# Branch gates with a 512-column product: the norm factor and the bias move from VectorE to GpSimd

## The chip, the cores and the metric

One Trainium2 chip, one core. The metric is device time in microseconds, the median of several runs of the whole program. PE is TensorE, ACT ScalarE, DVE VectorE, POOL GpSimd, SP the engine that issues most DMAs.

## What is computed

Three transformer blocks on 256 tokens of width 1024, in float32. The first one has two attention branches whose outputs are weighed by gates:

```python
h = _rmsnorm(x, g_mix[layer])
...
o_a = _stick_breaking_attention(...)
o_b = _diff_attention(q1, q2, k1, k2, vh, lam)
...
gates = jax.nn.sigmoid(jnp.einsum('bsd,de->bse', h, w_gate[layer]) + b_gate[layer])
gates = gates.reshape(b, s, N_BRANCH, D_MODEL)
merged = gates[:, :, 0] * br_a + gates[:, :, 1] * br_b
x = x + jnp.einsum('bsd,de->bse', merged, w_out[layer])
```

The change concerns the line with `gates`: 2048 output columns, computed as sixteen slabs of 128.

## The kernel before

The weights come as 319 slabs of 128x1024, through six slots (`stage`). For each slab ACT rounds it to a high half (`w_hi`, `next_hi`, L1058) and DVE subtracts to get the low half (`w_lo`, `next_lo`, L1490); the activations are split in the same way into `a_hi` and `a_lo`, which lie side by side in `a_pair`. A product is then the sum of three: high weights by high and by low activations, and low weights by high ones. `column_slab` (L496) does it with three matmuls of 256 columns for each of eight chunks, all into one half of a PSUM bank. `wide_slab` (L773), which the FFNs use, does the first two as one matmul of 512 columns over `a_pair`: the bank's first half then holds high by high plus low by high, the second half high by low, and someone has to add the halves. In the FFNs ACT copies the second half to SBUF (L1247) and DVE adds (L1701).

The gates run at L863 on PE: slab c goes to bank 4 or 2 in turn, and before slab c PE waits until the bank's earlier slab was taken out of it (`g_taken`). DVE (L1868 on) multiplies the bank by `rB`, the norm factor of each token, and adds the bias with a floor of -87 (L1883). After every second slab ACT turns two gates into sigmoids (`gates_out`, L1353: L1072, L1073, L1358), needed in the branch slabs that follow.

The differential attention is laid under the gates, as steps between slabs (`attend`, with the table `DA_AT`: head h starts at gate slab 1 + 3h). For a head, PE makes the scores (`da_scores`) after that slab; DVE takes row maxima (`da_max`, L1579, L1594); ACT the exponentials (`da_exp`, L1152); DVE normalizes and combines the two softmaxes (`da_probs`, L1600 to L1607) after its work on the gate of the next slab (for head 0 ahead of it, at slab 2); PE transposes (`da_turn`, L667) two slabs after the scores; then come the values, a sum of squares of the output (squared on POOL, L2094 and L2097), its norm on ACT, and the scaling on DVE (`da_out`, L1616). The order on each engine is that in which its block issues the instructions, with semaphores between the engines; no scheduler changes it.

Of the kernel before, what the change touches and what calls it, by code (L numbers as in the profile page):

```python
# [25 lines left out]
SLOTS = 6  # L26
# [28 lines left out]
V_BGATE = 64  # L55
# [40 lines left out]
def trunk(nc, xT_d, slab_d, vec_d, con_d, pos_d, out_d):  # L96
    f32, f32r, i32 = mybir.dt.float32, mybir.dt.float32r, mybir.dt.int32
    ALU, ACT = mybir.AluOpType, mybir.ActivationFunctionType
    with ExitStack() as ctx:
# [3 lines left out]
        def sem(name):  # L103
            return ctx.enter_context(nc.semaphore(name))
# [34 lines left out]
        def chunks(t, a, n):  # L139
# [66 lines left out]
                sem(n) for n in ("ds_done", "ds_taken", "ds_exp", "dp_ready", "dt_done", "dt_taken", "do_done",  # L206
                                 "do_taken", "dms_done", "dr_ready", "dn_ready", "do_hi", "do_lo"))
        down_done = sem("down_done")
        mix_ready, mhi_ready, mlo_ready = sem("mix_ready"), sem("mhi_ready"), sem("mlo_ready")
        acc_done = sem("acc_done")  # L210
        low_taken, gu_taken, gu_scaled, silu_ready, up_taken, ff_made, ffhi_ready, fflo_ready = (
# [38 lines left out]
        def half(b, i):  # L250
            return bank[b][:, i * TOK:(i + 1) * TOK]
# [192 lines left out]
        def _(pe):  # L444
# [418 lines left out]
            for c in range(16):  # L863
                n = GATE + c
                if c >= 2:
                    pe.wait_ge(g_taken, c - 1)
                else:
                    pe.wait_ge(qk_taken, 16)
                column_slab(n, n % SLOTS, half(GATE_BANK[c % 2], 0))
                if c < 2:  # L870
                    da_norm_sum(2 + c)
                attend(n)
# [157 lines left out]
        def _(act):  # L1030
# [329 lines left out]
            for c in range(16):  # L1360
                n = GATE + c
                if c == 1:
                    keys_factor(1)
                if c < 2:
                    pair_squares(2 + c)
                if c and c % 2 == 0:
                    gates_out(c - 2)
                next_hi(n)
                if c == 2:
                    queries_factor(1)  # L1370
                attend(n)
            gates_out(14)
            for s in range(8):
                attend(BRANCH + s)
                next_hi(BRANCH + s)
                j, side = branch(s)
                if side:
                    act.wait_ge(mix_ready, j + 1)
                    nc.scalar.activation(b_hi[:, 2 * j:2 * j + 2, :], gates[:, 2 * j:2 * j + 2, :], ACT.Copy
                                         ).then_inc(mhi_ready, 1)  # L1380
# [92 lines left out]
        def _(dve):  # L1473
# [394 lines left out]
            for c in range(16):  # L1868
                n = GATE + c
                attend_first(n)  # L1870
                next_lo(n)
                if c == 1:
                    normed_keys(1)
                if c == 2:
                    partners(0, 1)
                    da_probs(0)
                if c == 5:
                    partners(1, 1)
                dve.wait_ge(slab_done, n + 1)
                times(gates[:, c, :], half(GATE_BANK[c % 2], 0), rB[:, :]).then_inc(g_taken, 1)  # L1880
                dve.wait_ge(g_taken, c + 1)

                nc.vector.tensor_scalar(gates[:, c, :], gates[:, c, :], span(vec, V_BGATE + c, 1), -87.0, ALU.add,  # L1883
                                        ALU.max).then_inc(g_scaled, 1)
                attend(n)
                if c == 5:
                    rotated(0, 1)
                    rotated(1, 1)
# [173 lines left out]
        def _(pool):  # L2062
# [22 lines left out]
            for c in range(4):  # L2085
                for e in range(2):
                    pool.wait_ge(a_exp, 2 * c + e + 1)
                    below(soft_t[:, e, :]).then_inc(a_masked, 1)
            for h in range(4):

                pool.wait_ge(osq_made, h + 1)
                if h == 0:
# [2 lines left out]
                pool.wait_ge(osq_full, h + 1)  # L2095
                pool.wait_ge(do_taken, h + 1)
                nc.gpsimd.tensor_tensor(osq_lo, sq[:, 0:TOK], osq_hi.bitcast(f32), ALU.subtract).then_inc(osq_low, 1)  # L2097
            for m in range(1, 5):
                add_squares(add_index(m), 7, m + 1)
                if m == 1:  # L2100
# [134 lines left out]
```

## Time and profile before

| what | value |
|---|---|
| median of 3 runs | 1002.15 us (1001.6 to 1003.12) |
| the profiled execution | 1001.23 us |
| its span, from first to last instruction | 999.3 us |
| mean granted clock of TensorE | 0.998 |
| busy | PE 99%, DVE 73%, ACT 60%, POOL 6% |

The span lacks some 2 us of start and end that the time holds. The page's own sections give shares over the whole span; the gates take 57.6 us of it, from 95.7 to 153.3, so what happens there is read from timelines of that stretch.

### The profile page before, as it was taken

Reading aid. Unit: us, or ns where it says so; the run is one execution under the profiler, and the core shown is the slowest. Engines: PE = TensorE matmul, PEld = TensorE weight load, DVE = VectorE, ACT = ScalarE, POOL = GpSimd, SP = SyncE. Lnnn points to the kernel's source line nnn. Section 1 sums busy time; section 2 is a strip of 40 time slices with the busy share of each in tenths; the row PEclk is TensorE's granted clock in tenths of the full one; section 3 lists DMA queues with packets and bytes.
Section 4 is the critical chain, followed back from the end, with each engine's and each line's share of the span. In section 5 each row is a group of like instructions: output and inputs, shape, how many; then the busy total and the mean of one; then the engine's idle time right before and its main releaser. Section 6 shows DMA issues by size and latency. Waiting matters only on the chain.

```text
span 999.3 us, 17249 instructions
## 1 busy us (share of the span) xinstructions
PE 985.0 (99%) x6660; PEld 891.9 (89%) x6660; DVE 733.6 (73%) x1385; ACT 597.8 (60%) x1102; POOL 58.5 (6%) x78
## 2 busy tenths in 40 slices
PE   8999999999999999999999999999999999999996
PEld 7999989998888889999988888889989998888885
DVE  4668987798888548676498888647977688888644
ACT  5677785576566336565485555436668675565433
POOL 3011110020000002000020000002100010000000
PEclk9999999999999999999999999999999999999999
DMA  7743455456666764434546665753566456665731
GB/s 294 275 150 110 149 153 171 167 182 196 189 192 186 234 191 142 138 124 135 162 150 190 190 188 187 231 182 132 174 191 195 144 165 193 188 187 182 229 101 42
DMA packets 50928, 174.39 MB, mean 175 GB/s; under 512 B 6304, under 2 KB 8864, under 8 KB 50720
## 3 DMA queue, kind: packets, MB, share of 16 engines
q1 hardware_dynamic: 49664, 172.12, 54.3%
q10 hardware_dynamic: 1184, 1.18, 0.6%
q8 instruction: 53, 0.87, 0.4%
q14 instruction: 27, 0.22, 0.1%
HBM read 169.86 MB, written 1.05 MB: 171 GB/s over the span
## 4 chain that ended last, share of the span: by engine, by line
PE 95%; DVE 2%; ACT 1%; DMA 1%; issue 0%; SPq 0%; DVEq 0%; ACTq 0%
PE bank L446 93%; PE bank L667 1%; DMA stage<-slab_dram 1%; DVE w_lo L1490 1%; DVE arena L1483 0%; ACT w_hi L1058 0%; DVE soft_s L1579 0%; ACT soft_p L1152 0%; SPq L363 0%; DVE soft_p L1607 0%; DVE arena L1850 0%; ACT arena L1073 0%; DVE arena L1883 0%; ACT arena L1072 0%; DVE soft_p L1603 0%
## 5 line engine op out<-in xcount | busy, mean ns | idle before, releaser
L446 PE MATMUL bank<-a_pair,w_hi 128*128 128x512 f32 (+1 forms) x1968 | 532.6, 343 | 2.8 <-DVE w_lo L1490 2.1
L1490 DVE TENSOR_TENSOR w_lo<-stage,w_hi 128x1024 fp32r<-128x1024 f32 (+2 forms) x322 | 386.5, 1210 | 83.8 <-ACT w_hi L1058 79.2
L1058 ACT ACTIVATE w_hi<-stage 128x1024 fp32r<-128x1024 f32 (+2 forms) x314 | 325.6, 1043 | 165.7 <-PE bank L446 153.8
L446 PE MATMUL bank<-a_pair,w_lo 128*128 128x256 f32 x1488 | 416.8, 281 | 0.0
L446 PEld LDWEIGHTS bank<-a_pair,w_hi 128*128 128x128 f32 x1968 | 338.9, 189 | 51.3 <-DVE w_lo L1490 4.0
L446 PEld LDWEIGHTS bank<-a_pair,w_lo 128*128 128x128 f32 x1488 | 282.4, 190 | 0.0
L446 PE MATMUL bank<-arena_r,w_hi 128*128 128x256 f32 (+1 forms) x1024 | 237.0, 317 | 0.0
L446 PE MATMUL bank<-arena_r,w_lo 128*128 128x256 f32 x656 | 184.6, 282 | 0.0
L446 PEld LDWEIGHTS bank<-arena_r,w_hi 128*128 128x128 f32 x1024 | 168.7, 190 | 14.6 <-issue 1.4
L1247 ACT ACTIVATE arena<-bank 128x256 f32<-128x256 f32 x126 | 48.4, 384 | 136.4 <-PE bank L446 136.4
L446 PEld LDWEIGHTS bank<-arena_r,w_lo 128*128 128x128 f32 x656 | 125.0, 190 | 0.0
L1701 DVE TENSOR_TENSOR tmp<-bank,arena 128x256 f32<-128x256 f32 x126 | 53.5, 425 | 50.9 <-ACT arena L1247 44.2
L446 PE MATMUL bank<-ff_more,w_hi 128*128 128x512 f32 (+1 forms) x244 | 84.4, 392 | 0.0
L2076 POOL TENSOR_TENSOR sumsq<-sumsq,sq 128x256 f32<-128x256 f32 x47 | 38.1, 811 | 638.0 <-ACT sq L1079 587.2
L446 PE MATMUL bank<-ff_more,w_lo 128*128 128x256 f32 x240 | 67.3, 281 | 0.0
L1483 DVE TENSOR_TENSOR tmp<-tmp,rB 128x256 f32<-128x256 f32 x129 | 54.4, 422 | 4.3 <-ACT tmp L1238 2.2
L446 PEld LDWEIGHTS bank<-ff_more,w_hi 128*128 128x128 f32 x244 | 45.5, 188 | 10.7
L446 PE MATMUL bank<-w_hi,a_pair 128*128 128x256 f32 x256 | 47.7, 287 | 0.0
L446 PEld LDWEIGHTS bank<-ff_more,w_lo 128*128 128x128 f32 x240 | 45.4, 189 | 0.0
L446 PEld LDWEIGHTS bank<-w_hi,a_pair 128*128 128x128 f32 x256 | 39.8, 191 | 0.9 <-issue 0.6
L1579 DVE CUSTOM_DVE_ANT_0 soft_s<-bank,con 128x128 f32<-128x128 f32 x80 | 25.2, 355 | 15.5 <-PE bank L446 15.4
L446 PE MATMUL bank<-w_lo,a_pair 128*128 128x256 f32 x128 | 36.2, 282 | 0.0
(191 smaller groups left out, 776.2 us busy)
## 6 DMA issues: line engine op xcount, KB each, us to landing
stage<-slab_dram SPq DMA_DIRECT2D x319, 512.0 KB, 4.0
con<-con_dram SPq DMA_DIRECT2D x1, 1153.5 KB, 10.7
xT<-xT_dram SPq DMA_DIRECT2D x4, 256.0 KB, 5.4
arena<-arena ACTq DMA_DIRECT2D x1, 1024.0 KB, 8.8
arena<-tmp SPq DMA_DIRECT2D x32, 32.0 KB, 3.1
out_dram<-arena SPq DMA_DIRECT2D x3, 256.0 KB, 2.5
tmp<-arena SPq DMA_DIRECT2D x16, 16.0 KB
vec<-vec_dram SPq DMA_DIRECT2D x1, 213.5 KB, 11.5
```

The costliest lines, as they stand in the source:

```text
L446: return nc.tensor.matmul(out, lhsT, rhs, start=start, stop=True, skip_group_check=True)
L667: last = nc.tensor.transpose(b[:, i * P:(i + 1) * P], probs[:, i * P:(i + 1) * P], ident)
L1058: nc.scalar.activation(hi, raw, ACT.Copy).then_inc(hi_made, 1)
L1247: nc.scalar.activation(low[:, t % 4, :], half(GU_BANK[t % 8], 1), ACT.Copy).then_inc(low_taken, 1)
L1483: return nc.vector.tensor_tensor(out, a, b, ALU.mult)
L1490: return nc.vector.tensor_tensor(out, a, hi.bitcast(f32), ALU.subtract)
L1579: return nc.vector.tensor_tensor_reduce(out=s[:, cols], in0=b[:, cols], in1=con[:, mask + cols.start:mask + cols.stop], scale=1.0, scalar= ...
L1701: return nc.vector.tensor_tensor(out, half(GU_BANK[t % 8], 0), low[:, t % 4, :], ALU.add)
L2076: nc.gpsimd.tensor_tensor(sumsq[:, :], sumsq[:, :], sq[:, (i % 2) * TOK:(i % 2 + 1) * TOK], ALU.add).then_inc(sq_added, 1)
```

## The change

PE computes the gates with `wide_slab`. ACT copies the second half of the bank to `gates[:, c, :]` as soon as the slab is done (semaphore `g_low`), ahead of its `next_hi`. DVE adds the first half to it, one operation where it had two. POOL multiplies the sum by `rB` and adds the bias with the floor, in place; its work on the attention's squares becomes a function that is called between gates 3 and 4, 6 and 7, 9 and 10, 12 and 13. `gates_out` moves: it is called at odd slabs for the two gates up to c - 2, ahead of the copy; the last call comes after the first step of the branch slabs.

```diff
--- before.py
+++ after.py
@@ -206,6 +206,7 @@
                 sem(n) for n in ("ds_done", "ds_taken", "ds_exp", "dp_ready", "dt_done", "dt_taken", "do_done",
                                  "do_taken", "dms_done", "dr_ready", "dn_ready", "do_hi", "do_lo"))
         down_done = sem("down_done")
+        g_low, g_normed = sem("g_low"), sem("g_normed")
         mix_ready, mhi_ready, mlo_ready = sem("mix_ready"), sem("mhi_ready"), sem("mlo_ready")
         acc_done = sem("acc_done")
         low_taken, gu_taken, gu_scaled, silu_ready, up_taken, ff_made, ffhi_ready, fflo_ready = (
@@ -866,7 +867,7 @@
                     pe.wait_ge(g_taken, c - 1)
                 else:
                     pe.wait_ge(qk_taken, 16)
-                column_slab(n, n % SLOTS, half(GATE_BANK[c % 2], 0))
+                wide_slab(n, n % SLOTS, bank[GATE_BANK[c % 2]])
                 if c < 2:
                     da_norm_sum(2 + c)
                 attend(n)
@@ -1363,15 +1364,18 @@
                     keys_factor(1)
                 if c < 2:
                     pair_squares(2 + c)
-                if c and c % 2 == 0:
-                    gates_out(c - 2)
+                if c >= 3 and c % 2:
+                    gates_out(c - 3)
+                act.wait_ge(slab_done, n + 1)
+                nc.scalar.activation(gates[:, c, :], half(GATE_BANK[c % 2], 1), ACT.Copy).then_inc(g_low, 1)
                 next_hi(n)
                 if c == 2:
                     queries_factor(1)
                 attend(n)
-            gates_out(14)
             for s in range(8):
                 attend(BRANCH + s)
+                if s == 0:
+                    gates_out(14)
                 next_hi(BRANCH + s)
                 j, side = branch(s)
                 if side:
@@ -1876,12 +1880,9 @@
                     da_probs(0)
                 if c == 5:
                     partners(1, 1)
-                dve.wait_ge(slab_done, n + 1)
-                times(gates[:, c, :], half(GATE_BANK[c % 2], 0), rB[:, :]).then_inc(g_taken, 1)
-                dve.wait_ge(g_taken, c + 1)
-
-                nc.vector.tensor_scalar(gates[:, c, :], gates[:, c, :], span(vec, V_BGATE + c, 1), -87.0, ALU.add,
-                                        ALU.max).then_inc(g_scaled, 1)
+                dve.wait_ge(g_low, c + 1)
+                nc.vector.tensor_tensor(gates[:, c, :], half(GATE_BANK[c % 2], 0), gates[:, c, :], ALU.add
+                                        ).then_inc(g_taken, 1)
                 attend(n)
                 if c == 5:
                     rotated(0, 1)
@@ -2086,7 +2087,7 @@
                 for e in range(2):
                     pool.wait_ge(a_exp, 2 * c + e + 1)
                     below(soft_t[:, e, :]).then_inc(a_masked, 1)
-            for h in range(4):
+            def out_squares(h):
 
                 pool.wait_ge(osq_made, h + 1)
                 if h == 0:
@@ -2095,6 +2096,15 @@
                 pool.wait_ge(osq_full, h + 1)
                 pool.wait_ge(do_taken, h + 1)
                 nc.gpsimd.tensor_tensor(osq_lo, sq[:, 0:TOK], osq_hi.bitcast(f32), ALU.subtract).then_inc(osq_low, 1)
+
+            for c in range(16):
+                if c in (4, 7, 10, 13):
+                    out_squares(c // 3 - 1)
+                pool.wait_ge(g_taken, c + 1)
+                nc.gpsimd.tensor_tensor(gates[:, c, :], gates[:, c, :], rB[:, :], ALU.mult).then_inc(g_normed, 1)
+                pool.wait_ge(g_normed, c + 1)
+                nc.gpsimd.tensor_scalar(gates[:, c, :], gates[:, c, :], span(vec, V_BGATE + c, 1), -87.0, ALU.add,
+                                        ALU.max).then_inc(g_scaled, 1)
             for m in range(1, 5):
                 add_squares(add_index(m), 7, m + 1)
                 if m == 1:
```

ACT's order at gate slabs 5 and 6. Just ahead of these rows stand the exponentials of head 1 (L1152 before, L1153 now). L1072, L1073 and L1358 (now one more each) are `gates_out`, L1058 (L1059) is the high half of a weight slab, L1159 (L1160) takes the transposes of head 1. Before:

```order
L1152 ACTIVATE soft_p,small<-soft_s,small 128x256
L1058 ACTIVATE w_hi<-stage 128x1024 [waits loaded5,slab_done]
L1072 ACTIVATE arena<-arena 128x512 [waits g_scaled]
L1073 ACTIVATE arena<-arena 128x512 [waits act_step]
L1358 ACTIVATE arena<-arena 128x512 [waits act_step]
L1058 ACTIVATE w_hi<-stage 128x1024 [waits loaded0,slab_done]
```

Now; L1370 is the copy of the bank's second half, first for slab 5, then for slab 6:

```order
L1153 ACTIVATE soft_p,small<-soft_s,small 128x256
L1073 ACTIVATE arena<-arena 128x512 [waits g_scaled]
L1074 ACTIVATE arena<-arena 128x512 [waits act_step]
L1359 ACTIVATE arena<-arena 128x512 [waits act_step]
L1370 ACTIVATE arena<-bank 128x256 [waits slab_done]
L1059 ACTIVATE w_hi<-stage 128x1024 [waits loaded5,slab_done]
L1370 ACTIVATE arena<-bank 128x256 [waits slab_done]
L1059 ACTIVATE w_hi<-stage 128x1024 [waits loaded0,slab_done]
```

`gates_out` (the three rows of 128x512) now comes directly after the exponentials and ahead of the copy for slab 5; before, no row of this engine stood between the slab and DVE's work on it.

DVE's order at gate slab 5. Before; L1483 into `arena` is the multiply by `rB`, L1883 the bias, L1600 to L1607 are `da_probs` of head 1:

```order
L1490 TENSOR_TENSOR w_lo<-stage,w_hi 128x1024 [waits hi_made]
L1483 TENSOR_TENSOR tmp<-tmp,con 128x512 [waits rot_done1]
L1483 TENSOR_TENSOR arena<-bank,rB 128x256 [waits slab_done]
L1883 TENSOR_SCALAR arena<-arena,vec 128x256 [waits g_taken]
L1600 RECIPROCAL small<-small 128x4 [waits ds_exp]
L1601 TENSOR_SCALAR small<-small 128x2 [waits dve_step]
L1603 TENSOR_SCALAR soft_p<-soft_p,small 128x128
L1603 TENSOR_SCALAR soft_p<-soft_p,small 128x256
L1607 SCALAR_TENSOR_TENSOR soft_p<-soft_p,small 128x128 [waits dve_step]
L1607 SCALAR_TENSOR_TENSOR soft_p<-soft_p,small 128x256
```

Now; L1884 is the add, L1604 to L1611 are `da_probs`:

```order
L1494 TENSOR_TENSOR w_lo<-stage,w_hi 128x1024 [waits hi_made]
L1487 TENSOR_TENSOR tmp<-tmp,con 128x512 [waits rot_done1]
L1884 TENSOR_TENSOR arena<-bank,arena 128x256 [waits g_low]
L1604 RECIPROCAL small<-small 128x4 [waits ds_exp]
L1605 TENSOR_SCALAR small<-small 128x2 [waits dve_step]
L1607 TENSOR_SCALAR soft_p<-soft_p,small 128x128
L1607 TENSOR_SCALAR soft_p<-soft_p,small 128x256
L1611 SCALAR_TENSOR_TENSOR soft_p<-soft_p,small 128x128 [waits dve_step]
L1611 SCALAR_TENSOR_TENSOR soft_p<-soft_p,small 128x256
```

The bias row is gone, and the operation on the gate waits for `g_low`, which ACT's copy raises, in place of `slab_done`; `da_probs` stands behind it as before.

## Rows read from the trace of the kernel before

**Rows 1.** The page: busy time of each engine, and the chain that ended last.

```profile
PE 985.0 (99%) x6660; PEld 891.9 (89%) x6660; DVE 733.6 (73%) x1385; ACT 597.8 (60%) x1102; POOL 58.5 (6%) x78
...
PE 95%; DVE 2%; ACT 1%; DMA 1%; issue 0%; SPq 0%; DVEq 0%; ACTq 0%
```

**Rows 2.** View by windows, the stretch of the gate slabs: us, then busy us (instructions) by engine.

```profile
95.70:153.30 57.60, 55.49 (x449) 52.06 (x448) 52.26 (x125) 45.67 (x96) 7.10 (x9) 1.00 0.47 147
```

**Rows 3.** PE's timeline (start us, us): after each head's scores, and its transposes (L667).

```profile
112.22 0.92 PE L446 MATMUL bank<-soft_t,arena 128*128 128x256 f32 x4
...
118.73 0.49 PE L667 MATMUL bank<-con,soft_p 128*128 128x128 f32 x3
...
123.13 0.92 PE L446 MATMUL bank<-soft_t,arena 128*128 128x256 f32 x4
...
131.60 0.55 PE L667 MATMUL bank<-con,soft_p 128*128 128x128 f32 x3 [1.80 <-DVE soft_p L1607]
...
136.05 0.92 PE L446 MATMUL bank<-soft_t,arena 128*128 128x256 f32 x4
...
143.03 0.55 PE L667 MATMUL bank<-con,soft_p 128*128 128x128 f32 x3 [0.31 <-DVE soft_p L1607]
```

**Rows 4.** PE's timeline: first and next line after the first gate slab.

```profile
92.85 0.40 PE L446 MATMUL bank<-a_pair,w_hi 128*128 128x256 f32 x2
...
95.73 1.02 PE L446 MATMUL bank<-sq,con 128*128 128x512 f32 x2
```

**Rows 5.** PE's timeline: starts of two 512-column lines one FFN slab apart.

```profile
299.75 0.39 PE L446 MATMUL bank<-a_pair,w_hi 128*128 128x512 f32 x1
...
302.52 0.39 PE L446 MATMUL bank<-a_pair,w_hi 128*128 128x512 f32 x1
```

**Rows 6.** Groups of instructions by line; the POOL ones by source line (ns min/median/max).

```profile
L1247 ACT ACTIVATE arena<-bank 128x256 f32<-128x256 f32 x126 | 48.4, 384 | 136.4 <-PE bank L446 136.4
...
L1701 DVE TENSOR_TENSOR tmp<-bank,arena 128x256 f32<-128x256 f32 x126 | 53.5, 425 | 50.9 <-ACT arena L1247 44.2
...
L1883 DVE TENSOR_SCALAR arena<-arena,vec 128x256 f32<-128x256 f32 x16 | 6.1, 380 | 0.6
...
L2094 POOL TENSOR_TENSOR sq<-o_raw x4: 614/616/1383, 114.0 to 148.1; 128x256 f32<-128x256 f32 x4
...
L2066 POOL TENSOR_SCALAR_AFFINE_SELECT soft_t<-soft_t x8: 404/832/1511, 56.7 to 94.6; 128x256 f32<-128x256 f32 x8
```

**Rows 7.** ACT's timeline: ends of the exponentials (L1152), and `gates_out` between 117.12 and 119.04.

```profile
116.08 0.19 ACT L1152 ACTIVATION_READ_ACCUMULATOR soft_p<-soft_s,small 128x1 f32 x1
...
117.12 0.62 ACT L1072 ACTIVATE arena<-arena 128x512 f32<-128x512 f32 x1
...
119.04 1.05 ACT L1058 ACTIVATE w_hi<-stage 128x1024 fp32r<-128x1024 f32 x1
...
129.65 0.19 ACT L1152 ACTIVATION_READ_ACCUMULATOR soft_p<-soft_s,small 128x1 f32 x1
...
140.46 0.19 ACT L1152 ACTIVATION_READ_ACCUMULATOR soft_p<-soft_s,small 128x1 f32 x1
```

**Rows 8.** DVE's timeline: `da_probs` of head 1, two splits, first maximum of head 2.

```profile
116.78 0.17 DVE L1600 RECIPROCAL small<-small 128x4 f32<-128x4 f32 x1
...
117.70 0.75 DVE L1607 SCALAR_TENSOR_TENSOR soft_p<-soft_p,small 128x128 f32<-128x128 f32 x2
...
121.08 1.22 DVE L1490 TENSOR_TENSOR w_lo<-stage,w_hi 128x1024 fp32r<-128x1024 f32 x1
...
126.18 0.28 DVE L1579 CUSTOM_DVE_ANT_0 soft_s<-bank,con 128x128 f32<-128x128 f32 x1
...
138.91 1.76 DVE L1490 TENSOR_TENSOR w_lo<-stage,w_hi 128x1024 fp32r<-128x1024 f32 x1
```

**Rows 9.** POOL's timeline: the operation beside the second of these splits.

```profile
138.72 0.87 POOL L2097 TENSOR_TENSOR arena_r<-sq,arena_r 128x256 fp32r<-128x256 f32 x1
```

## Prediction

> **What bounds the kernel now.** Read the engine shares and the chain that ended last first [rows 1]: PE is busy 99% of the span and holds 95% of the chain. So the kernel ends sooner only if PE gets less to do, or waits less. DVE at 73% and ACT at 60% of the whole span look idle, but such a share is a mean over stages. The stretch of the sixteen gate slabs, taken alone from the view by windows, reads otherwise [rows 2]: in 57.6 us PE is busy 55.5, DVE 52.3 and ACT 45.7; POOL 7.1. There PE has 2.1 us of idle time, and DVE is nearly full.
>
> Where the 2.1 us lie is seen in PE's timeline [rows 3]. The differential attention runs under the gates, one head per three slabs: PE does the scores of head h after gate slab 1 + 3h, DVE takes the row maxima, ACT the exponentials, DVE normalizes (`da_probs`), and two slabs later PE transposes the result (L667). The transposes of head 2 stood 1.80 us idle, those of head 3 0.31 us, both released by the last line of `da_probs`. Head 1 came without a wait. These three loops decide the stage; everything behind it is PE's own pace, so what the stage gains or loses is kept.
>
> **The change, part by part.**
>
> *The wide form.* The first gate slab takes 95.73 - 92.85 = 2.88 us on PE [rows 4]; a slab of an FFN, already in the wide form, 302.52 - 299.75 = 2.77 us [rows 5]. Both have the same columns; 16 weight loads stand for 24. Sixteen times 0.11 is **1.8 us** off PE's own work.
>
> *ACT's new copy.* Sixteen more copies of 128x256 from PSUM; the FFN's copy of that form takes 0.38 us [rows 6], so 6.1 us on an engine with 57.6 - 45.7 = 11.9 us free. As a load it fits. What counts is its place. ACT's queue is in order, and in the changed order, at slab 5 (and 11), it is exponentials of the head, then `gates_out`, then the copy. DVE's add waits for that copy, and behind the add in DVE's queue stands `da_probs`, for which PE's transposes wait. Before, DVE's first gate operation waited for the slab alone, and `gates_out` ran beside `da_probs`.
>
> *The loops, one by one.* For each: from the end of the scores on PE, how long PE has work of its own until the transposes (two wide slabs save 0.22 us of it), and how long the others take.
>
> Head 1. PE: 118.73 - 112.22 = 6.51 [rows 3], now 6.3. The others: exponentials end at 116.08 + 0.19 = 116.27 [rows 7], 4.05 after the scores; `gates_out` 119.04 - 117.12 = 1.92 [rows 7]; the copy 0.38 [rows 6]; DVE's add 0.43 [rows 6]; `da_probs` 117.70 + 0.75 - 116.78 = 1.67 [rows 8]. Sum 8.45, so PE waits **2.2 us** where it waited none.
>
> Head 2. At slab 8 no `gates_out` stands ahead of the copy. PE: 131.60 - 1.80 - 123.13 = 6.67 [rows 3], now 6.45. The others: exponentials end at 129.84, 6.71 after the scores [rows 3, 7], as DVE began the maxima only at 126.18 [rows 8], 3.05 us after the scores; then 0.38 + 0.43 + 1.67. Sum 9.2 less what DVE catches up: three tensor-scalars of 0.38 [rows 6] fewer between, 1.1, of which new holds by POOL (below) eat part; I take 0.6, between 0 and 1.1. PE waits **2.1 us** in place of 1.80.
>
> Head 3. PE: 143.03 - 0.31 - 136.05 = 6.67, now 6.45 [rows 3]. The others: exponentials end at 140.65, 4.60 after [rows 7], then 1.92 + 0.38 + 0.43 + 1.67. Sum 9.0: PE waits **2.5 us** in place of 0.31.
>
> Head 0. Its `da_probs` stands ahead of the add, so nothing new precedes it. But PE comes up to 0.4 us earlier (four shorter slabs) and the probabilities do not: between 0 and 0.4, I take **0.3 us**.
>
> *DVE's part.* Multiply and tensor-scalar become one add: 16 x 0.38 = 6.1 us less DVE work [rows 6]; the add takes the time of the multiply. Beyond head 2's 0.6 us I give nothing for it, since DVE now stands and waits for the copy.
>
> *POOL's part.* Sixteen multiplies: POOL's 128x256 multiply of two SBUF operands takes 0.62 in the median [rows 6]. Sixteen tensor-scalars, of which no row shows one: the nearest with one source, the affine select of 256 elements, goes from 0.40 to 1.51 [rows 6]; I take 0.6, near the multiply, the row of the same shape. With four pairs of squares that is some 25 us of 57.6: beside other work, if it is on time. `gates_out` at slab 5 needs POOL's result of slab 3, asked for two slabs, 5.5 us, earlier: hidden. Without this cover each late result would stand in full in the chain above.
>
> *POOL against DVE.* This is not free. The split that DVE began at 138.91, under POOL's operation at 138.72 [rows 9], took 1.76 us, against 1.22 for the one at 121.08 [rows 8]: an operation on two SBUF operands on DVE is held by some 0.5 us when it meets one of POOL. The new multiply is released by the add, just as `da_probs` begins behind it. For heads 1 to 3 I add 0.3 us each, between 0 and 1.0 (both POOL operations met): **0.9 us**. The Trainium skill says it more strongly ("SBUF — State Buffer", section "Who interferes with whom"): the port pair of DVE and GpSimd is an exclusive lock, whoever issues first has it for the whole instruction and the other fully blocks. The rows agree: the split ran its own 1.22 us from about the end of POOL's operation, 139.59, on. By that rule all 32 POOL operations could hold DVE, which is the third rival below; my sum does not need it.
>
> SP, the loads and the splits: the copies push `next_hi` by 0.38 us, but a high half is made six slabs ahead of its use; the DMA queue's order is untouched. Nothing.
>
> **Sum.** New waits 0.3 + 2.2 + 2.1 + 2.5 + 0.9 = 8.0; less the old waits 2.1; less 1.8: **+4.1 us**. The profiled execution took 1001.23 and becomes 1005.3; it stands 0.9 below the median of the three runs, 1002.15, so against the median **1006.3 us**. With the terms at their ends, the waits go from 0 + 2.2 + 1.6 + 2.0 + 0 = 5.8 (head 3 with 0.5 less, as 4.60 holds other ACT work) to 0.4 + 2.2 + 2.7 + 2.6 + 3.0 = 10.9: 1004.1 to 1009.2 for this case alone.
>
> **The rivals.**
>
> *The copies come in time* (faster). It decides at slabs 5, 8 and 11: if the copy is done before DVE would reach its add, no wait is new, and the 6.1 us taken from DVE remove the lateness of 3.05 us that made the wait of 1.80. Then 1.8 + 2.1 = 3.9 us go: 998.3. For it: DVE is the fullest engine behind PE. Against it: ACT's order, in which 1.92 us of `gates_out` stand between exponentials and copy. 0.12.
>
> *One wait covers the next* (no change). A wait at head 1 lets ACT and DVE catch up, so that head 3, and the holds by POOL, cost nothing more: 0.3 + 2.2 + 2.1 - 3.9 = +0.7, 1002.9. For it: head 3 waited only 0.31 after head 2's 1.80. Against: each loop begins anew with PE's scores. 0.16.
>
> *DVE held by POOL becomes the bound.* If each of the 32 POOL operations holds DVE for its 0.62 us, DVE has 52.3 - 6.1 + 19.8 = 66 us of work in a stage of 57.6: 8.4 more, 1010.5. For it the lengthened split [rows 8]; against it DVE's many operations that read PSUM, and its idle time at the adds. By the rule of the skill's SBUF page named above the trace agrees on the hold, and no run here shows how often it meets. 0.14.
>
> *POOL falls behind.* With 1.51 us for its tensor-scalar, 0.62 for its multiply and a hold of up to one split, 1.2 us, for each gate, POOL needs 3.3 us, and its squares 0.3 per slab (two operations for four heads in sixteen slabs): the stage's whole 3.6 us per slab; then `gates_out` waits for POOL, 1.5 us at each of three heads: 4.5 more, 1010.8. 0.08.
>
> **How the numbers follow.** My case has 0.50. About 0.2%, 2 us, is what a measurement of this kernel tells from no change. Faster: the first rival, 0.12. Same: the second, and the low end of mine, 0.18. Slower: the rest, 0.70. The range leaves out the first rival and the top of the last two: 1001.5 to 1010.5.
>
> **What would show it.** Right: the gate stretch longer by 3 to 6 us; waits at L667 of about 2 us for heads 1, 2 and 3, released by `da_probs`; DVE's add idle before it until ACT's copy, by about 2 us at slabs 5 and 11; slabs 0.11 us shorter. Wrong: no L667 waits, or the waits at the slabs' own first matmuls (then the bank's release is the bound, not the heads); POOL's tensor-scalar over 1 us, or ACT idle before `gates_out` until POOL.

## The result, and the profile after

The changed kernel took 1006.79 us in the median of 10 runs (1003.46 to 1008.11), the kernel before 1001.88 on the same chip. The ratio on record is 1.0057 (the quotient of the two medians is 1.0049), with a 95% interval of [1.004, 1.0074]: slower, by 0.4 to 0.7%. The profiled execution took 1005.53 us, with a span of 1003.8.

The page of the changed kernel, engine shares and chain by engine, to be held against [rows 1]:

```profile
PE 985.8 (98%) x6532; PEld 886.2 (88%) x6532; DVE 730.8 (73%) x1369; ACT 602.8 (60%) x1118; POOL 99.2 (10%) x110
...
PE 95%; DVE 2%; ACT 1%; DMA 1%; issue 0%; SPq 0%; DVEq 0%; ACTq 0%
```

The chain reads as before. POOL went from 58.5 to 99.2 us, nearly 41 more. Nothing here says where the time went; that takes the stage's own timeline. It shows PE at the end of gate slab 0 (`sq,con`), at the transposes of heads 1 to 3 (L668, before L667), two steps of the slab behind head 2's, and the head 3 product that ends the stage (`arena_r`):

```profile
95.50 1.02 PE L447 MATMUL bank<-sq,con 128*128 128x512 f32 x2
...
120.58 0.55 PE L668 MATMUL bank<-con,soft_p 128*128 128x128 f32 x3 [2.00 <-DVE soft_p L1611]
...
133.77 0.55 PE L668 MATMUL bank<-con,soft_p 128*128 128x128 f32 x3 [0.77 <-DVE soft_p L1611]
...
134.74 0.40 PE L447 MATMUL bank<-a_pair,w_hi 128*128 128x512 f32 x1
...
136.86 0.40 PE L447 MATMUL bank<-a_pair,w_hi 128*128 128x512 f32 x1
...
147.27 0.55 PE L668 MATMUL bank<-con,soft_p 128*128 128x128 f32 x3 [2.62 <-DVE soft_p L1611]
...
156.89 0.28 PE L447 MATMUL bank<-arena_r 128*128 128x256 f32 x1
```

From 95.50 to 156.89 are 61.39 us. The same two landmarks stood 57.21 us apart before (95.73 and 152.94): **the stage is 4.18 us longer**. Head 1, which came without a wait, now waits 2.00; head 2 0.77 in place of 1.80; head 3 2.62 in place of 0.31 [rows 3]. Together 5.39 us of waits against 2.11.

One part of the loss is not a wait. Between the transposes of head 1 and of head 2, without the wait, lie 133.77 - 0.77 - 120.58 = 12.42 us; the same work from head 2 to head 3 takes 147.27 - 2.62 - 133.77 = 10.88. The view by windows around head 1's wait says why (columns: window, length, busy time of PE, PEld, DVE, ACT and POOL, granted clock, DMA share, GB/s):

```profile
118.60:120.60 2.00, 0.02 (x1) 0.02 (x1) 1.97 (x6) 1.56 (x3) 1.90 (x2) 1.00 0.00 0
120.60:122.00 1.40, 1.40 (x9) 1.31 (x10) 1.37 (x3) 0.83 (x2) 0.06 (x1) 0.92 0.00 0
122.00:124.00 2.00, 2.00 (x8) 1.71 (x8) 1.97 (x3) 1.84 (x5) 0.00 (x0) 0.50 0.00 0
124.00:125.00 1.00, 1.00 (x5) 0.81 (x5) 1.00 (x3) 0.38 (x1) 0.20 (x1) 0.50 0.00 0
```

After PE stood idle for 2 us, its granted clock went from 1.00 to 0.50, which is the lower level (1.2 GHz), for some 3 us. PE counts as fully busy there and does less: 12.42 - 10.88 = **1.54 us** lost to the clock.

So the stage's 4.18 us are 5.39 - 2.11 = 3.28 of new waits and 1.54 of clock, less 0.64 by which PE's own work is shorter (57.21 - 2.11 = 55.10 before, 61.39 - 5.39 - 1.54 = 54.46 now). This says where PE's time went, not what each part cost: had the clock stayed up, PE would have come to head 2's transposes earlier, and might have waited there instead. The filling below answers that.

Why head 1 waits is read in the queues. ACT from the end of head 1's exponentials (L1153) through `gates_out` (L1073 to L1359) to the copy (L1370):

```profile
115.62 0.19 ACT L1153 ACTIVATION_READ_ACCUMULATOR soft_p<-soft_s,small 128x1 f32 x1
115.72 0.62 ACT L1073 ACTIVATE arena<-arena 128x512 f32<-128x512 f32 x1
...
117.09 0.63 ACT L1359 ACTIVATE arena<-arena 128x512 f32<-128x512 f32 x1
117.63 0.37 ACT L1370 ACTIVATE arena<-bank 128x256 f32<-128x256 f32 x1
```

DVE over the same time, the add (L1884) and the normalization of head 1 behind it, then POOL's multiply beside it:

```profile
118.03 0.42 DVE L1884 TENSOR_TENSOR arena<-bank,arena 128x256 f32<-128x256 f32 x1 [1.75 <-ACT arena L1370]
118.37 0.17 DVE L1604 RECIPROCAL small<-small 128x4 f32<-128x4 f32 x1
118.57 0.71 DVE L1605 TENSOR_SCALAR small<-small 128x2 f32<-128x2 f32 x1
...
119.77 0.76 DVE L1611 SCALAR_TENSOR_TENSOR soft_p<-soft_p,small 128x128 f32<-128x128 f32 x2
```

```profile
118.54 0.72 POOL L2104 TENSOR_TENSOR arena<-arena,rB 128x256 f32<-128x256 f32 x1 [0.42 <-DVE arena L1884]
```

The exponentials are done at 115.81. DVE could normalize then, but its next instruction is the add, which stands idle for 1.75 us until the copy, and the copy stands behind `gates_out`. The probabilities are ready at 120.53, 4.72 us after the exponentials. Head 3 shows the same with an idle time of 2.47 at its add. The L1605 of 0.71 us lies beside POOL's multiply and ends with it (119.28 and 119.26); at head 0, and at all four heads before the change, it takes 0.23. So `da_probs` takes 120.53 - 118.37 = 2.16 us in place of 1.67 [rows 8]; from the same timeline, 2.22 at head 2 and 2.16 at head 3.

POOL's two operations in the groups of the same kernel over the whole span, and four lines of its waits between 95 and 165 us (columns: who waited for whom, us in total, times, longest):

```profile
L2106 POOL TENSOR_SCALAR arena<-arena,vec 128x256 f32<-128x256 f32 x16 | 20.9, 1308 | 1.6
L2104 POOL TENSOR_TENSOR arena<-arena,rB 128x256 f32<-128x256 f32 x16 | 20.0, 1252 | 16.3 <-DVE arena L1884 16.3
```

```profile
POOL arena L2104 <- DVE arena L1884: 16.3, 9, 4.1
DVE arena L1884 <- ACT arena L1370: 12.2, 9, 3.4
...
PE bank L668 <- DVE soft_p L1611: 5.4, 3, 2.6
...
ACT arena L1073 <- POOL arena L2106: 3.3, 3, 2.4
```

POOL takes 2.56 us for a gate, over twice the 1.22 that the prediction took from the nearest rows [rows 6]. It was still mostly in time: ACT waited for it 3.3 us in all.

### The profile page after: what moved, and what is told of

It reads as the page before. It is cut to its first block, busy times and chain, and to the rows that moved or that the text cites. A ratio compares the mean times of both kernels' runs of the same rounds, so it can differ in the third digit from the quotient of the medians.

```text
span 1003.8 us, 17025 instructions
## 1 busy us (share of the span) xinstructions
PE 985.8 (98%) x6532; PEld 886.2 (88%) x6532; DVE 730.8 (73%) x1369; ACT 602.8 (60%) x1118; POOL 99.2 (10%) x110
## 4 chain that ended last, share of the span: by engine, by line
PE 95%; DVE 2%; ACT 1%; DMA 1%; issue 0%; SPq 0%; DVEq 0%; ACTq 0%
PE bank L447 93%; PE bank L668 1%; DMA stage<-slab_dram 1%; ACT soft_p L1153 1%; DVE soft_s L1583 0%; DVE soft_p L1611 0%; DVE arena L1487 0%; ACT arena L1370 0%; SPq L364 0%; DVE small L1605 0%; DVE soft_p L1607 0%; DVE arena L1884 0%; DVE w_lo L1494 0%; ACT arena L1074 0%; ACT arena L1073 0%
## 5 line engine op out<-in xcount | busy, mean ns | idle before, releaser
L1059 ACT ACTIVATE w_hi<-stage 128x1024 fp32r<-128x1024 f32 (+2 forms) x314 | 325.4, 1043 | 156.9 <-PE bank L447 144.4
L447 PEld LDWEIGHTS bank<-a_pair,w_hi 128*128 128x128 f32 x1840 | 323.9, 189 | 56.2 <-DVE w_lo L1494 3.8
```

What stands on the lines that cost most here:

```text
L447: return nc.tensor.matmul(out, lhsT, rhs, start=start, stop=True, skip_group_check=True)
L1059: nc.scalar.activation(hi, raw, ACT.Copy).then_inc(hi_made, 1)
```

## The experiments

Three causes were set against each other. The **queue** theory (Q): the copy stands behind `gates_out` on ACT and ahead of the heads' normalization on DVE. The **port** theory (P): POOL's operations hold DVE. The **clock** theory (C): the waits lower PE's clock, which costs time of its own. "At the transposes" means PE at L668, for one head after the other.

What the unchanged rest of the program takes is not constant. From the end of the stage to the end of the span it was 843.2 to 845.8 us in four of the twelve profiled executions (the heads first, POOL left out, the filling, the bias alone on POOL) and 846.0 to 848.4 in the other eight, both kernels of the change among them. So single spans are not compared here. The stage's length and the waits carry the argument; the medians are given with their intervals, and a difference of 2 or 3 us between two kernels can come from the rest.

### The changed kernel once more

No edit.

> The changed kernel once more, on the chip of the three that follow, so that they have a common base: 4 to 6 us over the kernel before; waits at the transposes of heads 1 to 3 of about 2, 0.8 to 2.5 and 2.5 us, with the lower clock behind one of the first two of them.

Measured: 1006.38 us, ratio 1.0051 [1.0034, 1.0068]. The waits repeat to 0.2 us. Behind head 1's wait the clock falls again, and from head 1 to head 2 PE takes 133.72 - 0.60 - 120.61 = 12.51 us. Behind head 3's wait it falls too, as it did not in the first execution. PE's transposes of heads 1 to 3 and the end of the stage, then three windows, one behind head 1's wait and two behind head 3's:

```profile
120.61 0.89 PE L668 MATMUL bank<-con,soft_p 128*128 128x128 f32 x3 [2.00 <-DVE soft_p L1611]
...
133.72 0.55 PE L668 MATMUL bank<-con,soft_p 128*128 128x128 f32 x3 [0.60 <-DVE soft_p L1611]
...
147.24 0.55 PE L668 MATMUL bank<-con,soft_p 128*128 128x128 f32 x3 [2.63 <-DVE soft_p L1611]
...
158.42 0.40 PE L447 MATMUL bank<-arena_r 128*128 128x256 f32 x2
```

```profile
122.00:124.00 2.00, 2.00 (x7) 1.69 (x7) 1.97 (x3) 1.94 (x5) 0.00 (x0) 0.50 0.00 0
...
147.80:149.00 1.20, 1.20 (x6) 1.00 (x6) 1.20 (x3) 1.14 (x3) 0.26 (x1) 0.57 0.00 0
149.00:151.00 2.00, 2.00 (x9) 1.71 (x8) 0.79 (x1) 1.88 (x4) 1.90 (x2) 0.50 0.78 231
```

After the same wait of 2.6 us the clock stayed at 1.00 in the first execution, and the stretch from head 3 to the end took 156.89 - 147.27 = 9.62 us; here it fell to 0.50 and the stretch took 158.42 - 147.24 = 11.18, 1.56 more. The whole stage took 62.84 us, against 61.39. What the waits cost through the clock differs from one execution of the same program to the next.

### Taking the heads out from behind the copy

First edit: `da_probs` of heads 1 to 3 ahead of the add.

```diff
-                    if n - lag in at and (step is not da_probs or at[n - lag]):
+                    if n - lag in at and step is not da_probs:
...
+                if c in (5, 8, 11):
+                    da_probs((c - 2) // 3)
                 dve.wait_ge(g_low, c + 1)
                 nc.vector.tensor_tensor(gates[:, c, :], half(GATE_BANK[c % 2], 0), gates[:, c, :], ALU.add
...
```

> In the changed kernel da_probs of heads 1 to 3 is called ahead of the add of that slab; nothing else differs. Theory Q (the queues: the copy stands behind gates_out on ACT and ahead of da_probs on DVE): the waits at the transposes of heads 1 and 3 (2.00 and 2.62 us) fall under 0.4 us, head 2 keeps about 1 us from DVE's lateness, the lower clock after head 1 is gone; about 999.5 us, 2 to 3 us under the kernel before. Theory P (DVE held by POOL's operations): the POOL operations are all there, waits of 1.5 us or more stay, at best 1 us under the changed kernel, 1005 to 1007.

Measured: 999.64 us, ratio 1.0014 [0.9997, 1.0031]. The stage takes 56.77 us, 4.6 less than with the change alone. PE's waits after 112 us in this kernel:

```profile
130.73 0.55 PE L668 MATMUL bank<-con,soft_p 128*128 128x128 f32 x3 [1.65 <-DVE soft_p L1611]
...
141.91 0.55 PE L668 MATMUL bank<-con,soft_p 128*128 128x128 f32 x3 [0.30 <-DVE soft_p L1611]
153.14 0.47 PE L447 MATMUL bank<-arena_r,w_hi 128*128 128x256 f32 x2 [0.59 <-issue]
159.94 0.50 PE L447 MATMUL bank<-arena_r,w_hi 128*128 128x256 f32 x2 [0.81 <-DVE arena L1487]
```

Heads 1 and 3 are back to what they were before the change (no wait and 0.31), as the queue theory has it, and the clock stays at 1.00. From head 2 to head 3 PE takes 141.91 - 0.30 - 130.73 = 10.88 us, which is the price of that stretch at full clock. All of POOL's operations are still there, so this run also speaks against the port theory, which had the waits of the changed kernel stay: of those over 1.5 us only head 2's is left, and that one was there before the change. The gain over the kernel before that was expected did not come: two waits behind the stage, 0.59 and 0.81, take some of it. The second is POOL's lateness, seen at ACT's last `gates_out` but one (L1073) and DVE's last add (L1886):

```profile
155.41 0.63 ACT L1073 ACTIVATE arena<-arena 128x512 f32<-128x512 f32 x1 [3.63 <-POOL arena L2108]
```

```profile
157.73 0.43 DVE L1886 TENSOR_TENSOR arena<-bank,arena 128x256 f32<-128x256 f32 x1 [3.36 <-ACT arena L1370]
```

ACT waits 3.63 us for POOL's bias, the copy of slab 15 stands behind it, and DVE's add behind that.

Second edit: on ACT the copy ahead of `gates_out`.

```diff
-                if c >= 3 and c % 2:
-                    gates_out(c - 3)
                 act.wait_ge(slab_done, n + 1)
                 nc.scalar.activation(gates[:, c, :], half(GATE_BANK[c % 2], 1), ACT.Copy).then_inc(g_low, 1)
+                if c >= 3 and c % 2:
+                    gates_out(c - 3)
```

> In the changed kernel ACT's copy is issued ahead of gates_out at odd slabs; da_probs stays behind the add. Theory Q: 1.9 us of gates_out leave the loops of heads 1 and 3, whose waits fall from 2.00 and 2.62 to about 0.1 to 0.7 us each; head 2 waits 1 to 2.4 us; about 1001.5 us, between 1000 and 1003. Theory P: waits as in the changed kernel, 1006 to 1007.

Measured: 1001.03 us, ratio 1.0025 [1.0007, 1.0043]; the stage 59.06. At the transposes: head 1 none, head 2 2.51, head 3 0.69. After head 2's wait the granted clock is 0.76 in the window 130 to 135 us and 0.90 in the next. The transposes of heads 2 and 3:

```profile
131.95 0.55 PE L668 MATMUL bank<-con,soft_p 128*128 128x128 f32 x3 [2.51 <-DVE soft_p L1611]
...
145.13 0.55 PE L668 MATMUL bank<-con,soft_p 128*128 128x128 f32 x3 [0.69 <-DVE soft_p L1611]
```

Between them PE takes 145.13 - 0.69 - 131.95 = 12.49 us where it takes 10.88 at full clock. So the order on ACT alone removes head 1's wait and most of head 3's (2.00 and 2.62 with the change alone), from the other end of the same chain; head 2, ahead of whose copy no `gates_out` stands, is not helped by it, and waits a little more than the 1 to 2.4 us expected.

Both edits together:

> The changed kernel with da_probs of heads 1 to 3 ahead of the add and ACT's copy ahead of gates_out. Theory Q, with what e1_probs_first left: heads 1 and 3 without a wait, head 2 with 1.5 to 2.5 us, and the wait of 0.81 us in the branch slabs gone, since copy and add of slab 15 no longer stand behind the gates_out that waited 3.6 us for POOL; 0.5 to 2 us under the kernel before. If POOL's lateness in itself sets the end of the stage (theory L): the wait in the branch slabs stays, 1 to 2 us over before, as e1_probs_first.

Measured: 1001.68 us, ratio 1.0006 [0.999, 1.0022]; the stage 56.14, with one wait left at the transposes, head 2's 1.67, and two behind the stage, 0.49 and 0.40. The gain of 0.5 to 2 us over the kernel before that was expected did not come, and the wait behind the stage fell by half instead of going. The interval overlaps that of the first edit alone: the second adds nothing that can be told. With the clock at 1.00 all the way, the stage less its wait is 56.14 - 1.67 = 54.47 us, the same as the 54.46 worked out for the changed kernel.

### POOL left out

The multiply and the bias go back to DVE, behind the add; POOL does nothing for the gates.

```diff
                                         ).then_inc(g_taken, 1)
+                dve.wait_ge(g_taken, c + 1)
+                times(gates[:, c, :], gates[:, c, :], rB[:, :]).then_inc(g_normed, 1)
+                dve.wait_ge(g_normed, c + 1)
+                nc.vector.tensor_scalar(gates[:, c, :], gates[:, c, :], span(vec, V_BGATE + c, 1), -87.0, ALU.add,
+                                        ALU.max).then_inc(g_scaled, 1)
                 attend(n)
...
-                pool.wait_ge(g_taken, c + 1)
-                nc.gpsimd.tensor_tensor(gates[:, c, :], gates[:, c, :], rB[:, :], ALU.mult).then_inc(g_normed, 1)
-                pool.wait_ge(g_normed, c + 1)
-                nc.gpsimd.tensor_scalar(gates[:, c, :], gates[:, c, :], span(vec, V_BGATE + c, 1), -87.0, ALU.add,
-                                        ALU.max).then_inc(g_scaled, 1)
```

> The changed kernel with the multiply and the bias back on DVE, behind the add; POOL does nothing for the gates; copy and order on ACT as changed. Theory Q: the waits at heads 1 and 3 stay at 2 us or more, since the copy stands where it stood, and DVE has 0.9 us more per slab; 1006 to 1009. Theory P: DVE's lines have their plain length again, the waits fall to those of the kernel before or less, 1003 or under.

Measured: 1010.01 us in the median of four runs, ratio 1.0121 [1.0083, 1.0158]; somewhat over the 1006 to 1009 expected. PE's waits from 95 to 165 us, and three windows, each behind one of them:

```profile
PE bank L668 <- DVE soft_p L1611: 10.4, 4, 3.7
```

```profile
125.00:130.00 5.00, 5.00 (x27) 3.94 (x26) 4.86 (x9) 3.30 (x6) 0.00 (x0) 0.76 0.33 102
...
140.00:145.00 5.00, 5.00 (x30) 4.01 (x29) 2.81 (x7) 1.83 (x5) 0.00 (x0) 0.89 0.64 201
...
155.00:160.00 5.00, 5.00 (x22) 4.33 (x22) 2.72 (x6) 3.48 (x7) 0.00 (x0) 0.69 0.68 181
```

The four heads wait 0.88, 3.73, 2.07 and 3.70 us and the clock falls three times. Had POOL's holds been what the change costs, and more than what POOL takes off DVE (P), this kernel would have been the better one. It is the worst of all. Two things differ in it, though: the holds are gone, and DVE's multiply and bias stand in the heads' chain too, 0.42 and 0.35 us unheld. So it shows that POOL's part is worth more than its holds cost; that the holds don't make the waits is shown by the first edit above.

The same with the heads taken out of the chain (this edit and the first one above):

> As e1_probs_first, but the multiply and the bias stay on DVE and POOL does nothing for the gates: the wide product with its copy and its order repaired. Asked is what POOL's part is worth. DVE has 0.8 us more per slab than in e1_probs_first, and 0.45 more than before: head 1 without a wait, head 2 with 2.5 to 4 us from DVE's lateness, 2 to 5 us over the kernel before. If POOL's work costs more than it frees (theory P): faster than e1_probs_first.

Measured: 1004.57 us, ratio 1.004 [1.0022, 1.0058], against 1.0014 [0.9997, 1.0031] with POOL; the intervals overlap, the waits are plain. At the transposes 0.88, 0.34, 3.33 and 0.43 us, of which those of heads 2 and 3:

```profile
135.19 0.90 PE L668 MATMUL bank<-con,soft_p 128*128 128x128 f32 x3 [3.33 <-DVE soft_p L1611]
...
147.91 0.55 PE L668 MATMUL bank<-con,soft_p 128*128 128x128 f32 x3 [0.43 <-DVE soft_p L1611]
```

Head 2, the one that depends on DVE's load and not on the copy, waits 3.33 without POOL and 1.65 with it.

### Keeping PE busy through the waits

Ahead of the transposes of heads 1 to 3, PE does twelve more products of 256 columns into an unused bank; their results are used nowhere.

```diff
             def da_turn(h):
+                if h:
+                    for _ in range(12):
+                        mm(half(3, 0), a_hi[:, 0, 0:P], a_hi[:, 1, :], True)
                 pe.wait_ge(dp_ready, h + 1)
```

> The changed kernel with 12 extra matmuls of 128x256 into an unused bank ahead of the transposes of heads 1 to 3 (results unused, about 1.4 us each time), so that PE works during most of the wait. Asked is what the lower clock after head 1 cost. Theory Q: the clock stays at 1.00, but head 2's loop is set by DVE and ACT, so its wait, 0.77 us beside the lower clock, becomes about 1 us more than the filling, and the time stays within 1 us of the changed kernel, 1006 to 1007. If the lower clock is a cost of its own (theory C): 1.7 us less, 1005 or under.

Measured: 1002.11 us, ratio 1.003 [1.0014, 1.0046]. PE from the filling ahead of head 1's transposes on:

```profile
118.50 1.59 PE L447 MATMUL bank<-a_pair 128*128 128x256 f32 x12
120.78 0.55 PE L668 MATMUL bank<-con,soft_p 128*128 128x128 f32 x3 [0.69 <-DVE soft_p L1614]
```

All windows of the stage have a granted clock of 1.00, and the transposes come when they came in the changed kernel: 120.78, 133.73 and 147.21, against 120.58, 133.77 and 147.27. The stage takes 61.28 us against 61.39. So in the profiled execution of the changed kernel the lower clock behind head 1 cost nothing in the end: head 2's transposes waited for DVE either way, and the 1.54 us stood in place of a longer wait. Between heads 1 and 2 the filled kernel takes 133.73 - 0.65 - 120.78 = 12.30 us, of which 12.30 - 10.88 = 1.42 are filling; with the 0.65 that is a wait of 2.07 us for head 2, had nothing filled it. A fall behind head 3, as in the repeated execution, has no such wait behind it and adds its 1.56 us in full.

In the median this kernel is 0.27% better than the change alone (1.003 against 1.0057; the intervals overlap a little, and those of the repeated run, 1.0051 [1.0034, 1.0068], more). That is not shown to be the clock's doing (C): the two profiled stages are equally long, and the profiled executions differ behind the stage, 843.3 us here against 846.9. What the lower clock costs in the median stays open.

### The narrow form, and how much POOL should do

Now the change without its 512-column form: three products of 256 columns, no copy on ACT, DVE only moves the bank out, POOL multiplies and adds the bias.

```diff
-                wide_slab(n, n % SLOTS, bank[GATE_BANK[c % 2]])
+                column_slab(n, n % SLOTS, half(GATE_BANK[c % 2], 0))
...
-                act.wait_ge(slab_done, n + 1)
-                nc.scalar.activation(gates[:, c, :], half(GATE_BANK[c % 2], 1), ACT.Copy).then_inc(g_low, 1)
...
-                dve.wait_ge(g_low, c + 1)
-                nc.vector.tensor_tensor(gates[:, c, :], half(GATE_BANK[c % 2], 0), gates[:, c, :], ALU.add
-                                        ).then_inc(g_taken, 1)
+                dve.wait_ge(slab_done, n + 1)
+                nc.vector.tensor_copy(gates[:, c, :], half(GATE_BANK[c % 2], 0)).then_inc(g_taken, 1)
```

> The half of the change that moves work to POOL, alone: narrow products, no copy on ACT; DVE moves the bank to SBUF in one operation, POOL scales and adds the bias, gates_out as in the changed kernel. Theory Q: without the copy no loop is longer; DVE is freed of one operation per slab; head 2's wait 0.5 to 2 us; from 1.5 us under to 0.5 us over the kernel before. Theory P (DVE held by POOL): waits at heads 1 to 3 of 1.5 us or more, 3 us or more over before.

Measured: 1000.39 us, ratio 0.9984 [0.997, 0.9999]; the stage 55.89. The whole loss of the change is gone with the wide form and its copy, and its place is taken by a small gain: head 2 waits 1.01, the others not at all. The stage's PE work, 55.89 - 1.01 = 54.88, is 0.4 us more than the 54.47 of the kernel with both edits, and no more than the 56.77 - 1.65 - 0.30 = 54.82 of the one with the heads first. So the wide form is worth 0.4 us here at most, or 0.6 against the 55.10 of the kernel before.

DVE's move of the bank takes 0.41 us, its multiply of the same size 0.42. So DVE may multiply as it did before, and POOL does the bias alone:

```diff
-                nc.vector.tensor_copy(gates[:, c, :], half(GATE_BANK[c % 2], 0)).then_inc(g_taken, 1)
+                times(gates[:, c, :], half(GATE_BANK[c % 2], 0), rB[:, :]).then_inc(g_taken, 1)
...
                 pool.wait_ge(g_taken, c + 1)
-                nc.gpsimd.tensor_tensor(gates[:, c, :], gates[:, c, :], rB[:, :], ALU.mult).then_inc(g_normed, 1)
-                pool.wait_ge(g_normed, c + 1)
                 nc.gpsimd.tensor_scalar(gates[:, c, :], gates[:, c, :], span(vec, V_BGATE + c, 1), -87.0, ALU.add,
...
```

> Three matmuls of 256 columns per chunk and no copy on ACT, as in the kernel before; DVE multiplies the bank by rB itself, as before, and POOL does the bias alone; gates_out stands where the change put it. Against the kernel of experiment e7 this takes the multiply (0.73 to 1.72 us each) from POOL and leaves DVE as it was there (a multiply of 0.43 for a copy of 0.41). Theory Q (what cost time were the copy in the heads' chain and POOL's lateness; POOL's relief of DVE is a gain of its own): DVE has 16 x 0.38 = 6.1 us less than before, POOL 16 x 1.14 to 1.99 more, gates_out waits for POOL less than e7's 6.0 us in total; transposes of heads 0, 1 and 3 without a wait, head 2 at most e7's 1.01; 1 to 3 us under the kernel before, ratio 0.997 to 0.999, and not above e7's 0.9984 by more than 0.001. Theory P (POOL's holds on DVE eat the relief): head 2's wait stays at 1.5 or more, ratio 1.000 or above.

Measured: 996.42 us, ratio 0.9965 [0.9946, 0.9984]: **faster than both kernels**. PE at the transposes of heads 1 to 3 and the end of the stage, and ACT's wait for POOL:

```profile
118.79 0.49 PE L668 MATMUL bank<-con,soft_p 128*128 128x128 f32 x3
...
130.39 0.55 PE L668 MATMUL bank<-con,soft_p 128*128 128x128 f32 x3 [0.53 <-DVE soft_p L1609]
...
141.36 0.49 PE L668 MATMUL bank<-con,soft_p 128*128 128x128 f32 x3
...
151.21 0.40 PE L447 MATMUL bank<-arena_r 128*128 128x256 f32 x2
```

```profile
ACT arena L1073 <- POOL arena L2101: 1.2, 1, 1.2
```

The stage takes 151.21 - 95.81 = 55.40 us. Head 2's wait went from 1.80 to 0.53: the work taken from DVE comes out there, as the theory had it. The stage is 57.21 - 55.40 = 1.81 us shorter than before the change; the medians differ by 3.1 us (999.56 before, on this chip), and no run shows where the remaining 1.3 come from. With the kernel above the intervals overlap.

Last, the same kernel with `gates_out` where it stood before the change, at even slabs for the two gates just made:

> As e9, but gates_out stands where the kernel before had it (even slabs, for the two gates just made, ahead of the high half of the weights), so POOL's bias lies between DVE's multiply and ACT's sigmoids. At slabs 4 and 10 it stands ahead of a head's exponentials. If POOL's bias is what gates_out then waits for, ACT stands 1.1 to 2.0 us at each of those places (8 waits at most) and heads 1 and 3 get waits of up to 1 us at their transposes: 1 to 2 us above e9. If gates_out's place is of no consequence: within 0.5 us of e9 and ACT's waits for POOL under 3 us in total.

Measured: 998.01 us, ratio 0.999 [0.997, 1.0011]; the stage 56.90, 1.5 more than with the later place. At the transposes 0, 0.19, 0.72 and 0.56 us, and ACT waits for POOL in the gates' sigmoids:

```profile
ACT arena L1073 <- POOL arena L2100: 6.9, 6, 3.2
```

The waits are those that were expected if POOL's bias is what `gates_out` then waits for. By the stage's length, asking for POOL's result later is worth 1.5 us; the intervals of the two ratios still overlap.

## Why the prediction was right

The time came out as forecast: +4.9 us in the medians against a forecast of +4.1, and the likeliest case was the one that happened. By its own terms, for the profiled execution:

| term | predicted, us | measured, us |
|---|---|---|
| wide form, 16 slabs | -1.8 | -0.7 (0.10 at slab 0, 0.64 behind it) |
| head 0's wait | 0.3 | 0 |
| head 1's wait, with its hold | 2.2 + 0.3 | 2.00 |
| head 2's wait, with its hold | 2.1 + 0.3 | 0.77 |
| head 3's wait, with its hold | 2.5 + 0.3 | 2.62 |
| PE at its lower clock | not considered | 1.54 |
| old waits | -2.1 | -2.1 |
| sum | +4.1 | +4.1 |

**The queue was right.** The chain of exponentials, `gates_out`, copy, add and normalization is in the rows, and taking the heads out of it at either end takes their waits away. The adds' idle times of 1.75 and 2.47 us are the "about 2 us" that were named as the sign.

**The sum was better than its terms, which is luck.** The waits with their holds were to be 8.0 us. They came to 5.39, or 6.93 with the 1.54 of the lower clock: 1.1 too much was forecast. The wide form was to give 1.8 and gave 0.7: 1.1 too much again, with the other sign. The two errors cancel.

**Head 2's wait is not in its row.** It shows 0.77, not 2.1 to 2.4, and by that the sign of "about 2 us" failed. But PE came late to it by the 1.54 us of its lower clock, and 0.77 + 1.54 = 2.31; with PE kept busy it is 2.07. Where the heads stand ahead of the copy, DVE's lateness alone shows as 1.65. The loop was as forecast; what stood in it was not.

**The wide form was mis-sized.** 0.11 us per slab was taken from a slab of an FFN [rows 5]. Slab 0 did shrink from 2.88 to 2.78. But behind head 2's transposes six steps of a slab take 136.86 - 134.74 = 2.12 us, 0.353 each or 2.83 per slab; the FFN's 2.77 was 0.346 per step. Other slabs of the stage do go at the FFN's pace (six steps behind head 3's transposes, from 148.25 to 150.32, take 0.345 each), so this is a part of the reason and the rest stays open. PE's work in the fifteen slabs behind slab 0 is 0.64 us shorter, not 15 x 0.11 = 1.65. The row of another stage was not the price here.

**The clock was left out.** The prediction has no term for it. In the kernel before, the clock stays at 1.00 behind the wait of 1.80 us; here it fell behind the waits of 2.00 us in both executions and behind one of the two of 2.6. That did not spoil the forecast of the profiled execution, since head 2's wait covered the fall; in the repeated execution, with a fall behind head 3, the stage is 5.6 us longer than before and not 4.2.

**POOL's price was wrong, its place right.** Its tensor-scalar was taken at 0.6 us, within 0.40 to 1.51; it takes 1.31 in the mean and 1.14 at best. Its multiply was taken at 0.62 from a square, one tensor read twice; the multiply of two tensors takes 1.25 in the mean and 0.72 at best. The sign named for "wrong" (over 1 us) came true, but `gates_out` asks two slabs later, and only at the end does ACT stand 2.35 us. POOL's falling behind, a rival at 0.08, did not decide the change; it did cost part of the gain once the heads were out of the way.

**The holds are there and do not decide.** `da_probs` of heads 1 to 3 takes 2.16, 2.22 and 2.16 us in place of 1.67: a hold of 0.5 each, where 0.3 was forecast. The rule that was weighed was the exclusive lock of the Trainium skill ("SBUF — State Buffer", section "Who interferes with whom"). The trace agrees at head 1, where L1605 ends with POOL's multiply, 119.28 and 119.26. But DVE stood idle at its adds for 12.2 us in all, and the kernel without POOL's part is the slowest, 1.0121, so the third rival's sum, in which each operation holds DVE for its whole length, does not apply. Another rule speaks against POOL: "use DVE for elementwise" (the Trainium skill, "GPSIMD Engine Reference", section "Elementwise — side-by-side cycle accounting"). The rows agree that POOL is slower, 1.14 us and more for a bias that takes DVE 0.35; the time says otherwise, 0.9965 with the bias on POOL: DVE was the fullest engine behind PE [rows 2], and the bias had time.

**The first rival was nearly a kernel.** Its mechanism, work off DVE shortening head 2's wait, is what the bias-only kernel does; the wide form's copy is what kept it from happening here. The second rival did not come: head 3 waited 2.62 us though heads 1 and 2 had waited before it.

## What to carry to other kernels

Ask of each new wait what stands behind it in that engine's queue and what stands ahead of its releaser in the other's: the copy costs 0.37 us, and the queues around it made it 2 us for two heads. Move to a slow, idle engine only the operation that nobody needs soon, and ask for its result a step later; and let DVE, which has to take the bank out of PSUM in any case, do the multiply in the same operation. When PE is the bound, price a wait by its length and by the clock that may follow it, and ask whether a later wait covers that fall.

## What was not expected of the hardware

- The granted clock fell to 0.50 after idle times of PE of 2.00 us (both executions of the changed kernel) and of 2.63 (one of two: after 2.62 it stayed in the other). It also fell behind waits of 2.51 us (the copy first), 3.33 (the heads first, without POOL) and 2.07, 3.70 and 3.73 (POOL left out). It stayed at 1.00 behind the 1.80 us of the kernel before, and behind 1.65 and 1.67. By the subtraction used above each fall made PE 1.4 to 1.6 us slower: 12.29 us (the heads first, without POOL) to 12.51 from one head to the next in place of 10.88, and 11.18 from head 3 to the end in place of 9.62.
- POOL's one-source operation with a column of scalars, 128x256, takes 1.14 us at best, more than its multiply of two tensors, 0.72 at best.
- At the same granted clock of 1.00 the 512-column matmul has two paces. Its group in the window 420 to 560 us, which no edit touches, first in the changed kernel, then in the one with the bias on POOL (behind the count: busy us and mean ns of one, then the idle time before them):

```profile
L447 PE MATMUL bank<-a_pair,w_hi 128*128 128x512 f32 x135 | 47.8, 399 | 0.0
```

```profile
L447 PE MATMUL bank<-a_pair,w_hi 128*128 128x512 f32 x154 | 53.5, 392 | 0.0
```

In the kernel before it is 399 as well, and between 230 and 290 us all three have 391. Over the twelve profiled executions the pace goes with the length of the rest of the program: the four with 392 took 843.2 to 845.8 us from the end of the stage, the eight with 399 took 846.0 to 848.4. What chooses the pace stays open. It is why the last 0.3% can't be read from one profile.
